# A two-layer block on one core: the triangular inverse in 32x32 blocks, and 64-column products in two halves

## The chip, the cores and the metric

One core of a Trainium2 chip runs the whole kernel as one launch. The metric is device time in microseconds (us), the median of several runs. Engines are named as in the profile: PE (TensorE; PEld are its weight loads), DVE (VectorE), ACT (ScalarE), POOL (GpSimd), SP (SyncE, which issues the loads of weights).

## The reference, cut to what matters

256 tokens of width 1024 pass two layers in fp32. The first has an RWKV-7 mixer and a retention mixer side by side, then a convolutional feed-forward part; the second a Mamba-2 mixer, embeddings and windowed attention. Four places matter here.

- **RWKV-7 recurrence** (8 heads, head width 64). The reference steps through the tokens:

```python
sa = jnp.einsum('bhvk,bhk->bhv', S, -kk_t)
S = (S * w_t[:, :, None, :] + sa[..., None] * (kk_t * a_t)[:, :, None, :]
     + v_t[..., None] * k_t[:, :, None, :])
y = jnp.einsum('bhvk,bhk->bhv', S, r_t)
```

  The kernel does it in two chunks of 128 tokens. In a chunk the vectors `sa` solve a system with a unit triangular 128x128 matrix per head, so the inverse of I minus a strictly triangular matrix is needed for each of 8 heads, twice.
- **Retention**: per chunk of 128 tokens and head, scores q k^T with a decay mask, times v.
- **Mamba-2, diagonal part**: per chunk and head, a masked 128x128 matrix times a 128x64 block (32 heads).
- **Attention**: exponentiated scores (128x128 blocks) times values of 64 columns and a column of ones, 65 together.

## The kernel before, in words

Large products are made from a split: a weight unit of 128x2048 is loaded by SP, ACT writes its rounded upper part (`split_to`, L1321), DVE the rest (L1886), and PE adds three fp32r products (`mm3`, L440 to L442). The small products stay in plain fp32: each such call of `mm` is two weight loads and two passes in the trace, so one product counts as x2. Its operands' first partitions and sizes choose a tile of the PE array: 64 rows by 64 columns, or 64 rows by 128 columns, or all of it.

**Order around the change.** Each engine's program is written out by hand. PE works through `for n in range(2)` (the chunks), from L657 on. Between the small groups stand "dense" quarters (`dense(place)`): each is six fp32r products of 512 columns for the retention's input projection, laid there so that PE has work while ACT and DVE empty the banks. `QUARTERS` says how many stand at each place: one after each group of the inverse, five after the matrices, one or two after `rhs`, `sa` and `y`.

Per chunk:

1. Matrices (L661 to L675): for each of 8 heads two products of 64 rows and 256 columns into a bank (four banks in turn); DVE masks and writes them out (L2172). Two groups `L` (L674) make diagonal 64x64 blocks.
2. Start of the inverse: DVE masks the `L` banks (L2180), masks `invT` (L2183, two instructions of 64 partitions), and adds the unit matrix to both (L2187, 128x1024), which releases `inv_start`. POOL masks the pieces for each level into `lk`, two buffers in turn (L1230, two instructions of 64x512 a level).
3. Levels 1 to 5, on two 64x64 blocks per head held in `inv` and `invT`: `t1` (16 products, helper `blocks`, L654), a dense quarter while ACT copies `t1` to SBUF (L1517), then `x` and `xt` (32 products), a dense quarter while DVE adds them to `inv` and `invT` (L2194, L2197; at level 5 into `invTw`, L2200, L2201). Level 6 joins the two halves (L694, L700).
4. `rhs`, `sa`, `y` (L719, L728, L740, L741, and in the second chunk L716 and L736 of 128 columns): products of 64 columns on the whole array; the first chunk then makes the state (L748, L749).

In the second chunk DVE also does the rotary embedding of the retention's q and k between the levels (`rope_piece`: L2127 to L2131, L2145). Later come the retention scores (`scores_of`, L758), the Mamba diagonal (`diagonal`, L907, 8 groups of 8 products) and the attention's values (`values`, L1094, 12 groups of 4 products).

Of the kernel before, what the change touches and what calls it, by code (L numbers as in the profile page):

```python
# [27 lines left out]
P = 128  # L28
# [8 lines left out]
def constants():  # L37
# [10 lines left out]
    row6, col6 = row % 64, col[:, :64]  # L48
    for k in range(LEVELS - 1):
        same = (row6 >> (k + 1)) == (col6 >> (k + 1))  # L50
        parts[f"off{k}"] = same & (((col6 >> k) & 1) == 1) & (((row6 >> k) & 1) == 0)
    parts["off0L"] = (row6 >> 1 == col6 >> 1) & (col6 & 1 == 0) & (row6 & 1 == 1)
    parts["ident6"] = (row6 == col6)
# [104 lines left out]
def build(nc, io, out, where, ncols):  # L158
    ctx = ExitStack()
    with ctx:  # L160
# [77 lines left out]
        inv, invT, invTw, t1 = ar(23056, 8, 64), ar(23568, 8, 64), ar(24080, 8, P), ar(25104, 8, 64)  # L238
        both_inv, lk = ar(23056, 16, 64), ar(11280, 2, 8, 64)
# [181 lines left out]
        def _(pe):  # L421
# [226 lines left out]

            def blocks(key, bank, a, b):

                ps = take(pe, key, bank)
                for hd in range(8):
                    for r in (slice(0, 64), slice(64, P)):
                        last = mm(ps[r, 64 * hd:64 * hd + 64], a[r, hd, :], b[r, hd, :], start=True, stop=True)  # L654
                fill(last, key)

            for n in range(2):  # L657
# [3 lines left out]
                for hd in range(8):  # L661
                    p, o = hd // 2, hd % 2
                    r = slice(64 * o, 64 * o + 64)
                    ps = take(pe, ("m", n, hd), hd % 4)
                    mm(ps[:, 0:256], bt[r, p, n, :], zr[r, p, n, :], start=True, stop=True)
                    fill(mm(ps[:, 256:512], kt[r, p, n, :], zr[r, p, n, :], start=True, stop=True), ("m", n, hd))
                    if hd in (3, 5):
                        o = hd // 5
                        r = slice(64 * o, 64 * o + 64)
                        ps = take(pe, ("L", n, o), 4 + o)  # L670
                        for p in range(4):
                            for b in range(2):
                                c = slice(64 * b, 64 * b + 64)
                                last = mm(ps[c, 64 * p:64 * p + 64], zr[r, p, n, c], bt[r, p, n, c], start=True, stop=True)  # L674
                        fill(last, ("L", n, o))  # L675
# [3 lines left out]
                for k in range(1, LEVELS - 1):  # L679
                    pe.wait_ge(sem("lk_ready"), 10 * n + 2 * k)  # L680
# [7 lines left out]
                    blocks(("x", n, k), 0, invT, t1)  # L688
                    blocks(("xt", n, k), 1, t1, invT)
                    dense(("x", n, k))  # L690
                emptied(pe, ("x", n, 5))
                ps = take(pe, ("t1", n, 6), 4)
                for hd in range(8):
                    last = mm(ps[64:P, 64 * hd:64 * hd + 64], mats[0:64, hd, 0, 64:P], inv[0:64, hd, :], start=True, stop=True)  # L694
# [19 lines left out]
                for p in range(4):  # L714
                    if n:
                        mm(ps[:, P * p:P * p + P], zr[:, p, n, 0:P], s0[:, p, :], start=True, stop=False)  # L716
                    for o in range(2):
                        hd = 2 * p + o
                        last = mm(ps[:, 64 * hd:64 * hd + 64], mats[:, hd, 2, :], vrow[:, n, 64 * hd:64 * hd + 64],  # L719
                                  start=(n == 0), stop=(n == 0 or o == 1))  # L720
# [3 lines left out]
                if n == 0:  # L724
                    pe.wait_ge(sem("corner_clear"), 1)
# [8 lines left out]
                for p in range(4):  # L734
                    if n:
                        mm(ps[:, P * p:P * p + P], zr[:, p, n, P:2 * P], s0[:, p, :], start=True, stop=False)  # L736
                    for o in range(2):
                        hd = 2 * p + o
                        c = slice(64 * hd, 64 * hd + 64)
                        mm(ps[:, c], mats[:, hd, 3, :], vrow[:, n, c], start=(n == 0), stop=False)  # L740
                        last = mm(ps[:, c], mats[:, hd, 1, :], sa[:, c], start=False, stop=(n == 0 or o == 1))  # L741
# [11 lines left out]
            def scores_of(n):  # L753
                for o in range(2):
                    r = slice(64 * o, 64 * o + 64)
                    ps = take(pe, ("s", n, o), 2 + o)
                    for p in range(4):
                        last = mm(ps[:, P * p:P * p + P], kTr[r, p, P * n:P * n + P], qT[r, p, P * n:P * n + P],  # L758
                                  start=True, stop=True)
                    fill(last, ("s", n, o))  # L760
# [141 lines left out]
            def diagonal(g, n):  # L902
                pe.wait_ge(sem("wT_ready"), 4 * g + 2 * n + 2)
                ps = take(pe, ("yd", g, n), 6 + n)
                for e in range(8):
                    hd = 8 * g + e
                    last = mm(ps[:, 64 * e:64 * e + 64], wT[:, n, e, :], xd[:, n, 64 * hd:64 * hd + 64],  # L907
                              start=True, stop=True)
# [177 lines left out]
            def values(z):  # L1086
# [5 lines left out]
                for e in range(nh):  # L1092
                    for s in range(kt_):
                        last = mm(ps[:, 65 * e:65 * e + 65], aeT[:, z % 2, P * (kt_ * e + s):P * (kt_ * e + s) + P],  # L1094
                                  vv[:, s, 2 * u + o, :], start=(s == 0), stop=(s == kt_ - 1))
# [104 lines left out]
        def _(pool):  # L1200
# [25 lines left out]
            pool.memset(invTw[64:P, :, 0:64], 0.0).then_inc(sem("corner_clear"), 1)  # L1226

            def level_masked(n, k, r):

                pool.tensor_tensor(lk[r, k % 2, :, :], mats[r, :, 0, r], const(f"off{k}")[r].unsqueeze(1).broadcast_to([64, 8, 64]),  # L1230
                                   ALU.mult).then_inc(sem("lk_ready"), 1)

            for n in range(2):
                for k in range(1, LEVELS - 1):
                    if k == 1:
                        pool.wait_ge(sem("mats_ready"), 8 * (n + 1))
                        if n:
                            full(pool, ("t1", 0, 4))
                            full(pool, ("t1", 0, 5))
                    if k > 2:  # L1240
                        full(pool, ("t1", n, k - 2))
                    level_masked(n, k, slice(0, 64))
                    level_masked(n, k, slice(64, P))
# [50 lines left out]
        def _(act):  # L1294
# [217 lines left out]
            for n in range(2):  # L1512
                dense(("L", n), outs_behind=0)
                for k in range(1, LEVELS):
                    ps = full(act, ("t1", n, k))
                    r = slice(0 if k < 6 else 64, P)
                    empty(A(t1[r, :, :], ps[r, :].rearrange("p (a b) -> p a b", a=8), ACT.Copy), ("t1", n, k))  # L1517
# [338 lines left out]
        def _(ve):  # L1856
# [310 lines left out]
            for n in range(2):  # L2167
# [10 lines left out]
                for o in range(2):  # L2178
                    ps = full(ve, ("L", n, o))
                    empty(TT(iv[:, :, o, :], ps[:, 0:256].rearrange("p (a b) -> p a b", a=4),  # L2180
                             bc(const("off0L").unsqueeze(1), P, 4, 64), mul), ("L", n, o))
                for r in (slice(0, 64), slice(64, P)):
                    TT(invT[r, :, :], mats[r, :, 0, r], bc(const("off0")[r].unsqueeze(1), 64, 8, 64), mul) \  # L2183
# [612 lines left out]
```

## Time and profile before

| | us |
|---|---|
| three runs | 923.46, 923.89, 926.66 (median 923.89) |
| the profiled execution, its own time | 921.99 |
| its span | 920.1 |
| PE busy | 887.1 (96% of the span) |
| DVE busy | 671.3 (73%) |
| ACT busy | 505.7 (55%) |
| POOL busy | 88.2 (10%) |

Busy time is the time in which at least one instruction of the engine runs. Passes on different tiles of the array overlap, so the length of a group says more than the mean of one pass. In the timeline a row is a run of like instructions: start, length from the first start to the last end, engine, line, number of records.

### The profile page before, as it was taken

What the parts mean: (1) busy time and instruction counts of PE and PEld (TensorE: products, weight loads), DVE (VectorE), ACT (ScalarE), POOL (GpSimd) and SP (SyncE); (2) the same over time, 40 slices, a digit from 0 to 9 for tenths busy, and PEclk for the clock granted to TensorE, in tenths of its full rate; (3) what the DMA queues carried; (4) which work ended last, traced back from release to release, by engine and by line L of the source; (5) the groups of instructions that cost most, each with busy time, mean ns of one, the idle gap of its engine ahead of it and who ended that gap; (6) DMA issues with size and microseconds to landing.
All of it is one profiled execution on the core that took longest, in us unless ns stands there. A gap on an engine that the chain in (4) does not pass through costs nothing.

```text
span 920.1 us, 15340 instructions
## 1 busy us (share of the span) xinstructions
PE 887.1 (96%) x6217; PEld 768.1 (83%) x6217; DVE 671.3 (73%) x950; ACT 505.7 (55%) x722; POOL 88.2 (10%) x88
## 2 busy tenths in 40 slices
PE   6999999999999989999999899999999998999998
PEld 6997787798878779999988699988888886878777
DVE  6689729947777688888844777887686777776665
ACT  6863332334553567566634566764656566576553
POOL 6004405200000000000000000008220000000000
PEclk9999999999999989999999999999999999999999
DMA  9543322222644456655555365543323544522231
GB/s 306 171 137 98 116 93 93 93 92 92 226 167 147 170 191 205 201 183 188 196 194 193 101 189 184 184 137 122 108 93 108 179 149 176 190 92 92 92 116 68
DMA packets 80984, 136.43 MB, mean 148 GB/s; under 512 B 3958, under 2 KB 46546, under 8 KB 80913
## 3 DMA queue, kind: packets, MB, share of 16 engines
q1 hardware_dynamic: 78800, 130.91, 43.1%
q0 software_dynamic: 2112, 4.53, 1.5%
q8 instruction: 50, 0.82, 0.4%
q14 instruction: 22, 0.17, 0.1%
HBM read 134.38 MB, written 1.05 MB: 147 GB/s over the span
## 4 chain that ended last, share of the span: by engine, by line
PE 79%; DVE 9%; ACT 6%; issue 4%; DMA 2%; SPq 0%; DVEq 0%; ACTq 0%
PE bank L440 21%; PE bank L441 20%; PE bank L442 20%; PE bank L654 3%; PE bank L429 3%; DVE lower L1886 2%; ACT upper L1321 2%; PE bank L1094 1%; PE bank L899 1%; PE bank L907 1%; PE bank L1078 1%; DVE arena L2429 1%; DMA loaded<-in_w_in 1%; ACT arena L1420 1%; DVE arena L2183 1%
## 5 line engine op out<-in xcount | busy, mean ns | idle before, releaser
L1886 DVE TENSOR_TENSOR lower<-loaded,upper 128x2048 fp32r<-128x2048 f32 x122 | 280.8, 2305 | 122.8 <-ACT upper L1321 121.2
L1321 ACT ACTIVATE upper<-loaded 128x2048 fp32r<-128x2048 f32 x122 | 231.9, 1904 | 113.9 <-PE bank L442 93.2
L440 PE MATMUL bank<-xT_upper,upper 128*128 128x256 f32 (+1 forms) x664 | 187.0, 282 | 1.3 <-DVE xT_lower L1951 1.3
L441 PE MATMUL bank<-xT_lower,upper 128*128 128x256 f32 (+1 forms) x664 | 185.5, 279 | 0.0
L442 PE MATMUL bank<-xT_upper,lower 128*128 128x256 f32 (+1 forms) x664 | 185.4, 279 | 0.0
L440 PE MATMUL bank<-upper,xT_upper 128*128 128x512 f32 (+1 forms) x360 | 146.7, 408 | 4.7 <-DVE lower L1886 3.5
L442 PE MATMUL bank<-upper,xT_lower 128*128 128x512 f32 (+1 forms) x360 | 139.9, 389 | 0.0
L441 PE MATMUL bank<-lower,xT_upper 128*128 128x512 f32 (+1 forms) x360 | 139.3, 387 | 0.0
L440 PEld LDWEIGHTS bank<-xT_upper,upper 128*128 128x128 f32 (+1 forms) x664 | 125.8, 190 | 2.4 <-issue 2.2
L441 PEld LDWEIGHTS bank<-xT_lower,upper 128*128 128x128 f32 (+1 forms) x664 | 126.1, 190 | 0.2
L442 PEld LDWEIGHTS bank<-xT_upper,lower 128*128 128x128 f32 (+1 forms) x664 | 125.9, 190 | 0.1
L440 PE MATMUL bank<-upper,split_arena 128*128 128x512 f32 x296 | 121.0, 409 | 2.9 <-DVE split_arena L1951 2.1
L441 PE MATMUL bank<-lower,split_arena 128*128 128x512 f32 x296 | 117.5, 397 | 0.0
L442 PE MATMUL bank<-upper,split_arena 128*128 128x512 f32 x296 | 117.3, 396 | 0.0
L440 PEld LDWEIGHTS bank<-upper,xT_upper 128*128 128x128 f32 x360 | 67.8, 188 | 20.8 <-DVE lower L1886 4.6
L442 PEld LDWEIGHTS bank<-upper,xT_lower 128*128 128x128 f32 x360 | 67.8, 188 | 14.6
L441 PEld LDWEIGHTS bank<-lower,xT_upper 128*128 128x128 f32 x360 | 68.0, 189 | 12.3 <-issue 0.5
L1420 ACT ACTIVATE arena<-bank 128x512 f32<-128x512 f32 (+1 forms) x67 | 37.2, 584 | 62.0 <-PE bank L442 18.1
L440 PEld LDWEIGHTS bank<-upper,split_arena 128*128 128x128 f32 x296 | 55.9, 189 | 17.6 <-DVE lower L1886 2.1
L442 PEld LDWEIGHTS bank<-upper,split_arena 128*128 128x128 f32 x296 | 55.9, 189 | 13.6
L441 PEld LDWEIGHTS bank<-lower,split_arena 128*128 128x128 f32 x296 | 56.0, 189 | 12.5 <-issue 0.5
L429 PE MATMUL bank<-consts,arena 128*128 128x128 f32 (+2 forms) x333 | 49.6, 288 | 15.8 <-DMA arena<-in_norm_mix_pre 5.1
(347 smaller groups left out, 1128.3 us busy)
## 6 DMA issues: line engine op xcount, KB each, us to landing
loaded<-in_w_in SPq DMA_DIRECT2D x26, 1024.0 KB, 5.1
loaded<-in_ffn_w_up SPq DMA_DIRECT2D x22, 1024.0 KB, 5.1
loaded<-in_ssm_in_w SPq DMA_DIRECT2D x20, 1024.0 KB, 5.2
loaded<-in_ffn_w_down SPq DMA_DIRECT2D x11, 1024.0 KB, 4.9
loaded<-in_ssm_out_w SPq DMA_DIRECT2D x8, 1024.0 KB, 5.0
loaded<-in_ple_gate_w SPq DMA_DIRECT2D x8, 1024.0 KB, 5.1
loaded<-in_attn_in_w SPq DMA_DIRECT2D x8, 1024.0 KB, 5.2
loaded<-in_w_branch_ret SPq DMA_DIRECT2D x4, 1024.0 KB, 5.1
```

The source lines that it names most:

```text
L429: last = pe.transpose(ps[0:n, j * P:j * P + m], a, ident[0:m, 0:m])
L440: mm(out, a[0], b[0], start=start, stop=False)
L441: mm(out, a[0], b[1], start=False, stop=False)
L442: return mm(out, a[1], b[0], start=False, stop=stop)
L654: last = mm(ps[r, 64 * hd:64 * hd + 64], a[r, hd, :], b[r, hd, :], start=True, stop=True)
L899: last = mm(ps[:, P * e:P * e + P], later[:, z % 2, e, :], const("incl"), start=True, stop=True)
L907: last = mm(ps[:, 64 * e:64 * e + 64], wT[:, n, e, :], xd[:, n, 64 * hd:64 * hd + 64], start=True, stop=True)
L1078: last = mm(ps[:, w * e:w * e + w], aqT[r, u, nh * gh * n + e, P * n:P * n + P], akT[r, u, 0:w], start=False, stop=(e == nh - 1))
L1094: last = mm(ps[:, 65 * e:65 * e + 65], aeT[:, z % 2, P * (kt_ * e + s):P * (kt_ * e + s) + P], vv[:, s, 2 * u + o, :], start=(s == 0), sto ...
L1321: A(part(upper, PARTS, n), part(loaded, LOADS, n), ACT.Copy).then_inc(uppers, 1)
L1420: empty(A(dst, ps[0:part_, 0:w], func), key)
L1886: TT(part(lower, LOADS, n), part(loaded, LOADS, n), part(upper, PARTS, n).bitcast(F32), sub) \
```

## The change

- Levels 1 to 4 work on four 32x32 blocks per head (32 products where there were 16, each with 32 rows, 32 stationary and 32 moving columns), on the four diagonal tiles of the array; `lk`, `inv`, `invT` and the masks have 32 columns per head. POOL first copies the four diagonal 32x32 blocks to `diag`, and DVE waits for that. POOL's masks are one instruction of 128x256 a level.
- Level 5 joins pairs of 32-blocks: 16 products of 32x32 in each of `t1`, `x`, `xt`, from `mats`, `inv` and `invT`.
- POOL copies the blocks after level 4 into `inv6` (2 copies) and `invTw` (4 copies); DVE copies what level 5 made. PE waits for POOL's six copies (`inv_placed`) ahead of level 6.
- Products of 64 or 65 columns on the whole array (`rhs`, `sa`, `y`, `diagonal`, `values`; with them those of 128 columns in the second chunk's `rhs` and `y`) become two, each with half of the stationary columns (`halves`).
- The matrices and the retention scores are issued for two heads in turn, on the upper and the lower 64 rows; the two `L` groups become one of 32 products, 64 rows by 32 columns.
- The table of constants is 288 columns narrower (664 KB before).

```diff
+            def halves(ps, c, a, b, start, stop):
+                mm(ps[0:64, c], a[:, 0:64], b, start=start, stop=stop)
+                return mm(ps[64:P, c], a[:, 64:P], b, start=start, stop=stop)
...
             def blocks(key, bank, a, b):
                 ps = take(pe, key, bank)
                 for hd in range(8):
-                    for r in (slice(0, 64), slice(64, P)):
-                        last = mm(ps[r, 64 * hd:64 * hd + 64], a[r, hd, :], b[r, hd, :], start=True, stop=True)
+                    for r in fourths:
+                        last = mm(ps[r, 32 * hd:32 * hd + 32], a[r, hd, :], b[r, hd, :], start=True, stop=True)
                 fill(last, key)
...
+                for p in range(4):
+                    mps = [take(pe, ("m", n, 2 * p + o), (2 * p + o) % 4) for o in range(2)]
+                    for o in range(2):
+                        mm(mps[o][:, 0:256], bt[rows_[o], p, n, :], zr[rows_[o], p, n, :], start=True, stop=True)
+                    for o in range(2):
+                        fill(mm(mps[o][:, 256:512], kt[rows_[o], p, n, :], zr[rows_[o], p, n, :], start=True, stop=True),
+                             ("m", n, 2 * p + o))
+                    if p == 1:
+                        lps = [take(pe, ("L", n, o), 4 + o) for o in range(2)]
+                        for p4 in range(4):
+                            for b in range(4):
+                                c = slice(32 * b, 32 * b + 32)
+                                for o in range(2):
+                                    last = mm(lps[o][c, 32 * p4:32 * p4 + 32], zr[rows_[o], p4, n, c], bt[rows_[o], p4, n, c],
+                                              start=True, stop=True)
...
-                for k in range(1, LEVELS - 1):
-                    pe.wait_ge(sem("lk_ready"), 10 * n + 2 * k)
+                for k in range(1, 5):
+                    pe.wait_ge(sem("lk_ready"), 4 * n + k)
...
+                pairs = ((fourths[0], fourths[1]), (fourths[2], fourths[3]))
+                for hd in range(8):
+                    for a, b in pairs:
+                        last = mm(ps[b, 32 * hd:32 * hd + 32], mats[a, hd, 0, b], inv[a, hd, :], start=True, stop=True)
...
+                dense(("x", n, 5))
+                pe.wait_ge(sem("inv_placed"), 6 * n + 6)
...
-                    last = mm(ps[:, 64 * hd:64 * hd + 64], invTw[:, hd, :], rhs[:, 64 * hd:64 * hd + 64],
-                              start=True, stop=True)
+                    c = slice(64 * hd, 64 * hd + 64)
+                    last = halves(ps, c, invTw[:, hd, :], rhs[:, c], True, True)
...
+                for r in fourths:
+                    pool.tensor_copy(diag[r, :, :], mats[r, :, 0, r]).then_inc(sem("diag_ready"), 1)
+                pool.wait_ge(sem("diag_ready"), 4 * n + 4)
+                for k in range(1, 5):
                     if k > 2:
                         full(pool, ("t1", n, k - 2))
+                    pool.tensor_tensor(lk[:, k % 2, :, :], diag[:, :, :], const(f"off{k}").unsqueeze(1).broadcast_to([P, 8, 32]),
+                                       ALU.mult).then_inc(sem("lk_ready"), 1)
...
+                for r in fourths[0:2]:
+                    pool.tensor_copy(inv6[r, :, r], inv[r, :, :]).then_inc(sem("inv_placed"), 1)
+                emptied(pool, ("xt", n, 4))
+                if n:
+                    full(pool, ("sa", 0))
+                for r in fourths:
+                    pool.tensor_copy(invTw[r, :, r], invT[r, :, :]).then_inc(sem("inv_placed"), 1)
...
+                ve.wait_ge(sem("diag_ready"), 4 * n + 4)
+                TT(invT[:, :, :], diag[:, :, :], bc(const("off0").unsqueeze(1), P, 8, 32), mul).then_inc(sem("inv_masked"), 1)
...
-                TT(both_inv, both_inv, bc(const("ident6").unsqueeze(1), P, 16, 64), add).then_inc(sem("inv_start"), 1)
+                TT(both_inv, both_inv, bc(const("ident5").unsqueeze(1), P, 16, 32), add).then_inc(sem("inv_start"), 1)
```

## Rows read from the trace of the kernel before

**Rows 1.** The page: span, busy time by engine, chain that ended last.

```profile
span 920.1 us, 15340 instructions
...
PE 887.1 (96%) x6217; PEld 768.1 (83%) x6217; DVE 671.3 (73%) x950; ACT 505.7 (55%) x722; POOL 88.2 (10%) x88
...
PE 79%; DVE 9%; ACT 6%; issue 4%; DMA 2%; SPq 0%; DVEq 0%; ACTq 0%
```

**Rows 2.** Busy time by stretch: second chunk's levels, Mamba's diagonal, attention.

```profile
core 0: us, PE busy (x) PEld busy (x) DVE busy (x) ACT busy (x) POOL busy (x), PEclk, DMA share, GB/s
...
153.00:185.00 32.00, 32.00 (x551) 25.85 (x545) 29.06 (x34) 10.77 (x11) 11.15 (x7) 1.00 0.31 100
...
634.00:712.00 78.00, 76.11 (x455) 64.94 (x454) 57.74 (x86) 45.74 (x77) 18.63 (x16) 1.00 0.32 108
...
812.00:880.00 68.00, 66.28 (x366) 52.93 (x365) 42.42 (x101) 43.50 (x76) 0.00 (x0) 1.00 0.24 78
```

**Rows 3.** Timeline of PE, second level of the first chunk.

```profile
93.46 1.15 PE L654 MATMUL bank<-arena 64*64 64x64 f32 x32
94.54 0.50 PE L440 MATMUL bank<-upper,xT_upper 128*128 128x512 f32 x1
94.88 0.39 PE L441 MATMUL bank<-lower,xT_upper 128*128 128x512 f32 x1
...
95.80 0.40 PE L442 MATMUL bank<-upper,xT_lower 128*128 128x512 f32 x1
96.13 2.08 PE L654 MATMUL bank<-arena 64*64 64x64 f32 x64
98.14 0.50 PE L440 MATMUL bank<-upper,xT_upper 128*128 128x512 f32 x1
98.48 0.39 PE L441 MATMUL bank<-lower,xT_upper 128*128 128x512 f32 x1
```

**Rows 4.** Timeline of PE: a group on one 64x64 tile; two column tiles, same rows.

```profile
118.53 1.14 PE L694 MATMUL bank<-arena 64*64 64x64 f32 x16
...
75.28 0.68 PE L674 MATMUL bank<-arena 64*64 64x64 f32 x16
```

**Rows 5.** Timeline of PE's weight loads, the 10 ns from 87.18.

```profile
87.18 0.14 PEld L654 LDWEIGHTS bank<-arena 64*64 64x64 f32 x2 [0.78 <-DVE arena L2187]
```

**Rows 6.** Timeline of PE around `sa` of the first chunk, whole array.

```profile
126.69 0.39 PE L442 MATMUL bank<-upper,xT_lower 128*128 128x512 f32 x1
126.92 1.89 PE L728 MATMUL bank<-arena 128*128 128x64 f32 x16
128.62 0.48 PE L440 MATMUL bank<-upper,xT_upper 128*128 128x512 f32 x1
128.94 0.40 PE L441 MATMUL bank<-lower,xT_upper 128*128 128x512 f32 x1
```

**Rows 7.** Mamba's diagonal (all), one group of attention's values, one of the scores.

```profile
L907 PE MATMUL bank<-arena 128*128 128x64 f32 x128 | 15.2, 272 | 0.0
...
820.37 1.11 PE L1094 MATMUL bank<-arena 128*128 128x65 f32 x8
...
221.82 1.71 PE L758 MATMUL bank<-arena 64*128 64x128 f32 x16
```

**Rows 8.** DVE: ahead of the inverse (timeline), second chunk's levels (groups: busy, mean ns).

```profile
79.78 1.29 DVE L2172 TENSOR_TENSOR arena<-bank,consts 128x512 f32<-128x512 f32 x2 [0.50 <-PE bank L666]
...
85.02 2.10 DVE L2187 TENSOR_TENSOR arena<-arena,consts 128x1024 f32<-128x1024 f32 x1
...
L2194 DVE TENSOR_TENSOR arena<-arena,bank 128x512 f32<-128x512 f32 x5 | 3.4, 681 | 1.9 <-PE bank L654 1.9
...
L2128 DVE TENSOR_TENSOR lora<-arena,small 128x256 f32<-128x256 f32 x4 | 3.8, 952 | 0.0
...
L2129 DVE TENSOR_TENSOR lora<-arena,small 128x256 f32<-128x256 f32 x4 | 1.7, 416 | 0.0
```

**Rows 9.** Timeline of POOL: masks for levels 1 and 2, and for level 5.

```profile
81.34 6.92 POOL L1230 TENSOR_TENSOR arena<-arena,consts 64x512 f32<-64x512 f32 x4 [65.42 <-DVEq L2176]
...
100.97 2.63 POOL L1230 TENSOR_TENSOR arena<-arena,consts 64x512 f32<-64x512 f32 x2 [3.27 <-PE bank L654]
```

More of the change, by code:

```diff
@@ L47, in constants @@
     parts["blkret"] = np.repeat(parts["blk"][:, ::64], P, axis=1)
[L48 to L53, printed above, removed]
+    row5, col5 = row % 32, col[:, :32]
+    for k in range(LEVELS - 2):
+        same = (row5 >> (k + 1)) == (col5 >> (k + 1))
+        parts[f"off{k}"] = same & (((col5 >> k) & 1) == 1) & (((row5 >> k) & 1) == 0)
+    parts["off0L"] = (row5 >> 1 == col5 >> 1) & (col5 & 1 == 0) & (row5 & 1 == 1)
+    parts["ident5"] = (row5 == col5)
     lg = np.log1p(-np.exp2(-5.0 - np.arange(8)))
@@ L647, in _ @@
             pe.wait_ge(sem("decayed"), 1)
+            fourths = [slice(32 * g, 32 * g + 32) for g in range(4)]
             def blocks(key, bank, a, b):
@@ L660, in _ @@
                     turns(("kbT", 1), 3, [bt[:, p, 0, :] for p in range(4)])
[L661 to L675, printed above, removed]
+                rows_ = (slice(0, 64), slice(64, P))
@@ new lines, in _ @@
+                for p in range(4):
[13 more added lines that the diff above has]
+                                              start=True, stop=True)
+                                    if p4 == 3 and b == 3:
+                                        fill(last, ("L", n, o))
@@ L693, in _ @@
                 for hd in range(8):
[L694 removed]
+                    last = mm(ps[64:P, 64 * hd:64 * hd + 64], mats[0:64, hd, 0, 64:P], inv6[0:64, hd, :], start=True, stop=True)
                 fill(last, ("t1", n, 6))
@@ L735, in _ @@
                     if n:
-                        mm(ps[:, P * p:P * p + P], zr[:, p, n, P:2 * P], s0[:, p, :], start=True, stop=False)
+                        halves(ps, slice(P * p, P * p + P), zr[:, p, n, P:2 * P], s0[:, p, :], True, False)
                     for o in range(2):
@@ L739, in _ @@
                         c = slice(64 * hd, 64 * hd + 64)
-                        mm(ps[:, c], mats[:, hd, 3, :], vrow[:, n, c], start=(n == 0), stop=False)
-                        last = mm(ps[:, c], mats[:, hd, 1, :], sa[:, c], start=False, stop=(n == 0 or o == 1))
+                        halves(ps, c, mats[:, hd, 3, :], vrow[:, n, c], n == 0, False)
+                        last = halves(ps, c, mats[:, hd, 1, :], sa[:, c], False, n == 0 or o == 1)
                 fill(last, ("y", n))
@@ L753, in scores_of @@
             def scores_of(n):
[L754 to L758, printed above, removed]
+                ps = [take(pe, ("s", n, o), 2 + o) for o in range(2)]
+                for p in range(4):
+                    for o in range(2):
+                        r = slice(64 * o, 64 * o + 64)
+                        last = mm(ps[o][:, P * p:P * p + P], kTr[r, p, P * n:P * n + P], qT[r, p, P * n:P * n + P],
                                   start=True, stop=True)
-                    fill(last, ("s", n, o))
+                        if p == 3:
+                            fill(last, ("s", n, o))
             def outputs_of(n):
@@ L906, in diagonal @@
                     hd = 8 * g + e
-                    last = mm(ps[:, 64 * e:64 * e + 64], wT[:, n, e, :], xd[:, n, 64 * hd:64 * hd + 64],
-                              start=True, stop=True)
+                    last = halves(ps, slice(64 * e, 64 * e + 64), wT[:, n, e, :], xd[:, n, 64 * hd:64 * hd + 64], True, True)
                 fill(last, ("yd", g, n))
```

88 lines of the change are left out of this document (50 added, 38 removed).

## The prediction

> **What bounds the kernel now.** I read the page first: PE is busy for 887.1 of 920.1 us and holds 79% of the chain that ended last [rows 1]. Then the stretches: in the second chunk's levels PE is busy for all of 32 us, in Mamba's diagonal for 76 of 78, in attention for 66 of 68, at a granted clock of 1.00 (2.4 GHz) [rows 2]. So time taken off PE's small groups comes off the end, as long as ACT, DVE and POOL keep up. Of these DVE is near its limit in one place: 29.06 of 32 us in the second chunk's levels [rows 2].
>
> Then the timeline, for the length of the groups. In a level `t1` (x32) stands at 93.46 and the next dense product at 94.54; `x` and `xt` (x64) run from 96.13 to 98.14 [rows 3]. Less the last pass's 0.22 us, 64 passes take 2.08 - 0.22 = 1.86 us, 29 ns each. A group on one tile, x16 in 1.14 us, gives (1.14 - 0.22) / 15 = 61 ns a pass, the first gap being longer; so one 64x64 tile takes a pass about every 58 ns and two tiles share that time fully. The same holds for two column tiles on the same rows: x16 in 0.68 us is 31 ns a pass [rows 4]. Loads of two tiles start almost together: two of them, each 0.13 us, cover 0.14 us in the first 10 ns of a group [rows 5]. Changing the form of tile costs something: from the start of the last dense product (95.80) to that of the second one after (98.48) are 2.68 us; two ordinary steps are 0.46, the 64 passes 64 x 29.2 = 1.87 us, which leaves 0.35 us for going in and out.
>
> Whole-array products of 64 columns: from 126.69 to 128.94 are 2.25 us, less 0.46 is 1.79 us for 16 passes, 112 ns a pass with no visible switch [rows 6]. That is four times the pace of two 64-tiles, for twice the array.
>
> **The change, part by part.** The sum is made against the profiled execution (921.99 us, 1.9 below the median of 923.89); the savings are then taken off the median.
>
> (1) *Levels 1 to 4.* Twice as many passes, half as wide, on four tiles instead of two. No row has a 32-column pass. Bounds: if a tile's pass shrinks with its columns, it takes 32 ns (128 stationary columns take 112 ns [rows 6], 64 take 58.4, so 64 columns are 53.6 and some 5 ns are fixed; 32 columns are 27 and 5), four tiles give 8 ns a pass, and `t1` takes 0.51 us instead of 0.93, `x`+`xt` 1.02 instead of 1.87: 1.27 us off a level. If each pass keeps the 29.2 ns that it has on average now [rows 3], `t1` takes 1.87 and `x`+`xt` 3.74: 2.80 us more a level. I take the first, because the pace of rows 3 and rows 4 is exactly a tile's own time divided by the tiles, and the loads of rows 5 start a few ns apart; nothing there looks like a limit per instruction. For 8 levels: -10.2 us (bound +22.4).
>
> (2) *Level 5.* As many passes as before, 32 wide on two tiles: 16 ns each, again -1.27 us a chunk, -2.5 in all; 0 if the pass does not shrink. Level 6 stays.
>
> (3) *Halves.* 8 products become 32 passes at 29.2 ns, 0.93 + 0.35 for the switch = 1.28 against 1.79: -0.5 us. Nearest row is x16 of two column tiles on 64 rows [rows 4]; on 128 rows it is not shown. `rhs` and `sa` of both chunks: 4 x 0.5. The two `y` have 16 products: 3.57 becomes 1.87 + 0.35, -1.35 each. The 128-column products of the second chunk stay at two loads' worth of time (112 ns a pass, two at a time). Together -4.7. Mamba's diagonal, x128 in 15.2 us [rows 7], is 8 such groups: -4.1. Attention: a group of x8 takes 1.11 us [rows 7], 8 x 112 = 0.90 without the tail; as halves 0.48 + 0.35, some 0.1 less, and part of it is taken up by the wait for ACT's exponentials: -1.2 for 12 groups. Sum -10.0. The bound on the other side, if halves do not share: 32 x 58.4 + 0.35 = 2.22 instead of 1.79 for 8 products, 12 us more over all sites.
>
> (4) *Scores by two heads in turn.* x16 in 1.71 us [rows 7] is one group after the other at 107 ns; with upper and lower rows in turn about 0.95: -0.75 a chunk, -1.5 (bounds 0 and -1.6).
>
> (5) *Matrices and `L`.* PE waits for DVE's masking there (the last two, to 81.07, after a wait of 0.50 [rows 8]). What shrinks is `L`, twice 0.68 us [rows 4] to one group of about 0.5, and part of the interleaving: -0.75 a chunk, -1.5 (bounds 0 and -2.6).
>
> (6) *Start of the inverse.* Now DVE ends the 128x1024 add at 87.12 [rows 8], and PE's loads had been idle for 0.78 us by 87.18 [rows 5]. In the new kernel POOL's four copies come first. No copy of POOL is in the trace; its masks of 64x512 take 1.3 us each when alone (2.63 for two) and 1.7 beside DVE (6.92 for four) [rows 9], 2.6 to 3.4 ns a column, so a copy of 256 columns costs 0.3 to 0.9 us. I take 0.5: from 81.1 the copies end at 83.2, `invT` (0.42) and the add of 512 columns (0.69) at 84.5 (84.5 to 86.1 with 0.9). PE comes there at 87.18 less (5), about 86.2: hidden by the five dense quarters (5 x 6 x 0.23 = 6.9 us), without them it would be 3 us a chunk. Counted 0.
>
> (7) *POOL's six copies ahead of level 6.* They start when DVE has added level 4 and take 6 x 0.5 = 3 us, at most 5.4; PE has three dense quarters (4.1 us), `t1`, `x` and `xt` of level 5 (1.5 + 0.7) ahead of the wait: 6.3 us. Counted 0. Queued behind PE's wait are level 6 and all of `rhs`, so each us over would be lost.
>
> (8) *DVE in the second chunk.* PE's stretch of 32 us shrinks by 5 x 1.27 to 25.7. DVE's 29.06 loses 0.27 for each of nine adds (681 against 416 ns for half the columns [rows 8]), 2.4 us, and part of what POOL's port use costs it: the same instruction takes 952 ns on average at L2128 beside POOL and 416 at L2129 mostly after it [rows 8], and POOL was busy for 11.15 us [rows 2] where about half is left. That makes 23.5 to 24.5 us of 25.7, 93% full. What is late next is DVE's add of `x` ahead of `t1`: I give back 1.5 us there (0 to 4), and 1.5 more for waits of ACT and DVE in all the other shortened groups (0 to 3).
>
> (9) The narrower table: 0.
>
> Sum: -10.2 - 2.5 - 10.0 - 1.5 - 1.5 + 3.0 = -22.7, so 923.9 - 22.7 = **901 us**.
>
> **Rivals.**
>
> *A pass of 32 columns takes as long as one of 64.* Then four tiles give 58.4 / 4 = 14.6 ns a pass; twice the passes at half the time each cancels: (1) and (2) are 0, and less is given back: 923.9 - 13.0 + 1 = 912. For it: the 5 fixed ns are worked out from two sizes, and neither is 32. Against it: nothing in the rows. The Trainium skill ("TensorEngine Tiling (Array Packing)", Instruction Overhead) speaks for it: a matmul has some 60 cycles of overhead, and one should not take the tiling factor from a dimension that is already small. No row here tests that rule.
>
> *PE cannot be fed fast enough (the slower side).* Now at most one load and one pass are asked for in 29.2 ns; (1) asks for four times that, in groups of 64 and 128 passes. With p ns for a pass, 24 products of 64 passes change by 24 x (64p - 934) ns: nothing at 14.6, +16 us at 25, +22.4 at 29.2. With the other parts (-13) the whole breaks even at p = 23 and is over 0.5% slower from p = 26; at 29.2 it is 923.9 - 13.0 + 22.4 = 933. Against it: rows 5, two loads within a few ns, but two are not a stream. The Trainium skill ("TensorE: Matmul & The Clock Gate", "Wait - 56ns, not 53.3ns?") says that start-to-start never drops below about 25 ns; its p would give an estimate of about 927, and rows 5 differ from it for two different tiles.
> Between 10 and 23 ns the same mechanism gives 904 to 924.
>
> *Halves over all 128 rows do not share their time.* Then (3) is +12 instead of -10: 901 + 22 = 923, no change. Against it: two column tiles at 31 ns a pass [rows 4].
>
> **How the numbers follow.** 0.5% (4.6 us) is about what a measurement of this kernel can tell from no change. Forecast (897 to 907): 0.45. Pass that does not shrink: 0.15. Feeding between: 0.15, half of it faster by over 0.5%. Feeding at 26 ns or over: 0.12. Halves not shared: 0.06. Others, of both signs (a granted clock that drops once more or less, a stall behind POOL): 0.07. Faster 0.71, same 0.15, slower 0.14. The range goes from 895, with nothing given back, to 928, which leaves out the slow end alone.
>
> **What would show it.** In the timeline `x`+`xt` should be x128 in about 1.2 us (2.1 for the first rival, over 3.5 for the second), `t1` x64 in 0.7; a diagonal group x32 in about 1.15 instead of x16 in 1.9; the scores' x16 in 1.1. The second chunk's levels should be 6 us shorter with DVE over 90% busy, and PE should show no wait for POOL. Wrong would be a group of 128 passes above 1.9 us, or an idle PE of over 1 us a level behind DVE or POOL.

## The result and the profile after

The new kernel takes 912.97 us (median of 4 runs, 911.06 to 913.91) against 923.67 for the one before (4 runs): 10.7 us less, ratio 0.989, 95% interval 0.987 to 0.991. The prediction was 901, with a range of 895 to 928: the direction and the range held, but less than half of the 22.7 us came. The profiled run took 913.91 us, its span is 912.1. Single executions differ before the change even begins: the transposes ahead of the matrices start at 72.22 us in the profile before and at 74.42 in this one, so a difference of 1 to 2 us between two profiles says nothing by itself.

The page, as [rows 1], with the queue that fetches instructions (before: 50 packets, 0.82 MB):

```profile
span 912.1 us, 17764 instructions
...
PE 865.1 (95%) x7417; PEld 740.6 (81%) x7417; DVE 650.8 (71%) x948; ACT 503.2 (55%) x722; POOL 73.4 (8%) x96
...
q8 instruction: 59, 0.97, 0.4%
...
PE 79%; DVE 7%; ACT 6%; issue 5%; DMA 2%; SPq 0%; DVEq 0%; ACTq 0%
```

PE is busy for 22 us less, but its share falls. The same two stretches as in [rows 2] (columns as there):

```profile
153.00:185.00 32.00, 27.96 (x896) 21.24 (x894) 23.25 (x34) 9.30 (x11) 4.31 (x7) 1.00 0.29 99
634.00:712.00 78.00, 73.03 (x551) 59.80 (x551) 58.45 (x89) 46.51 (x79) 15.97 (x12) 0.98 0.33 112
```

In the levels PE now idles for 4 us of 32, where it idled for none, and DVE, feared at 93%, is busy for 23.25. The timeline of PE, levels 1 and 2 of the first chunk, answers to [rows 3]:

```profile
88.57 0.75 PE L661 MATMUL bank<-arena 32*32 32x32 f32 x64
89.25 0.50 PE L445 MATMUL bank<-upper,xT_upper 128*128 128x512 f32 x1
...
90.83 1.36 PE L661 MATMUL bank<-arena 32*32 32x32 f32 x128
92.12 0.50 PE L445 MATMUL bank<-upper,xT_upper 128*128 128x512 f32 x1
...
93.71 0.59 PE L661 MATMUL bank<-arena 32*32 32x32 f32 x45
97.23 0.53 PE L661 MATMUL bank<-arena 32*32 32x32 f32 x19 [2.94 <-issue]
97.69 0.80 PE L445 MATMUL bank<-upper,xT_upper 128*128 128x512 f32 x1
```

Level 1 is what was forecast: `t1` is 0.68 us long (1.08 before), `x` and `xt` 1.29 (2.01). In level 2 PE stops after 45 of 64 passes for 2.94 us and waits for nothing that the profile shows ("issue"). The second chunk, same view, L661 alone:

```profile
153.46 1.31 PE L661 MATMUL bank<-arena 32*32 32x32 f32 x128
156.29 0.62 PE L661 MATMUL bank<-arena 32*32 32x32 f32 x49
157.84 0.32 PE L661 MATMUL bank<-arena 32*32 32x32 f32 x15 [0.93 <-issue]
159.70 1.13 PE L661 MATMUL bank<-arena 32*32 32x32 f32 x106
161.76 0.38 PE L661 MATMUL bank<-arena 32*32 32x32 f32 x22 [0.94 <-issue]
163.66 0.75 PE L661 MATMUL bank<-arena 32*32 32x32 f32 x64
165.94 1.31 PE L661 MATMUL bank<-arena 32*32 32x32 f32 x128
168.77 0.38 PE L661 MATMUL bank<-arena 32*32 32x32 f32 x23
170.47 0.56 PE L661 MATMUL bank<-arena 32*32 32x32 f32 x41 [1.32 <-issue]
172.56 0.89 PE L661 MATMUL bank<-arena 32*32 32x32 f32 x80
174.30 0.61 PE L661 MATMUL bank<-arena 32*32 32x32 f32 x48 [0.86 <-issue]
```

The waits of PE over the whole run sum these up:

```profile
PE bank L661 <- issue: 7.6, 6, 2.9
```

Six stops: two of the first chunk's eight groups are broken in two (the other stop, of 0.61 us, is in `x` and `xt` of level 4), and four of the second chunk's. Taken from start to next product, the 16 groups of levels 1 to 4 last 25.2 us; unbroken they would last 8 x (0.68 + 1.24) = 15.4, before they lasted 8 x (1.08 + 2.01) = 24.7. Of the 9.8 us between 25.2 and 15.4 the stops are 7.6; the rest is mostly the restart behind each and one group at the lower clock (`x` and `xt` of level 2, 1.86 us instead of 1.24). So all that the narrow tiles save in levels 1 to 4 is lost again. Before the long stop the DMA engines are busy for 80% of the time, and behind it the clock is at its lower level (1.2 GHz) for 5.7 us (windows, columns as [rows 2]):

```profile
91.31:94.86 3.55, 2.98 (x146) 2.29 (x133) 2.66 (x3) 1.60 (x1) 0.00 (x0) 1.00 0.80 259
...
97.20:102.90 5.70, 5.67 (x154) 4.50 (x155) 0.77 (x2) 0.98 (x2) 0.73 (x1) 0.50 0.02 6
```

**Where the stops stand.** Count PE's own instructions in the program's order: an fp32 product is four (two loads, two passes), a split product or a transpose two, a wait one. (A half pass below is a load whose pass comes after the stop.) A level has 410 (218 before). The second level's `t1` begins at instruction 1637; 45 passes further is 1727. The others come out in the same way: 2599 + 2 x 76 = 2751; 4188 + 2 x 49.5 = 4287; 4330 + 2 x 106.5 = 4543; 5009 + 2 x 23 = 5055; 5150 + 2 x 80.5 = 5311. All six leave the remainder 191 when divided by 256. The number of packets fits blocks of that size as well: PE's loads, passes and waits in the trace are 15,174, or 59.3 times 256, and q8 has 59 packets of 16,384 bytes; before they were 12,761, or 49.8 times 256, and 50 packets. Each stop ends 1.2 to 1.5 us after such a packet has ended. Where two stops follow each other on neighbouring blocks, 256 instructions last 161.76 - 157.84 = 3.92 us and 174.30 - 170.47 = 3.83 us. At 3.85 us for 256, a level of 410 takes 6.2 us at the least; the level of before took 6.27, and the four of the second chunk now take 25.2 us, 6.3 each. That is the theory the runs had to test: **PE's instructions come in blocks of 256, asked for one block ahead, one in about 3.85 us at most.** (Pairs of stops in the later profiles lie 3.28 to 4.20 us apart, so the last number is a middle and not a limit.)

### The profile page after: what moved, and what is told of

The parts are those of the page before. It is cut to its first block, busy times and chain, and to the rows that moved or that the text cites. A ratio compares the mean times of both kernels' runs of the same rounds, so it can differ in the third digit from the quotient of the medians.

```text
span 912.1 us, 17764 instructions
## 1 busy us (share of the span) xinstructions
PE 865.1 (95%) x7417; PEld 740.6 (81%) x7417; DVE 650.8 (71%) x948; ACT 503.2 (55%) x722; POOL 73.4 (8%) x96
## 4 chain that ended last, share of the span: by engine, by line
PE 79%; DVE 7%; ACT 6%; issue 5%; DMA 2%; SPq 0%; DVEq 0%; ACTq 0%
PE bank L445 22%; PE bank L447 21%; PE bank L446 21%; PE bank L429 3%; ACT upper L1358 3%; DVE lower L1925 2%; PE bank L440 2%; PE bank L661 2%; PE bank L928 1%; PE bank L1106 1%; DVE arena L2469 1%; DMA h<-in_x 1%; ACT arena L1457 1%; DMA loaded<-in_kv_w 1%; ACT arena L1841 1%
## 5 line engine op out<-in xcount | busy, mean ns | idle before, releaser
L447 PEld LDWEIGHTS bank<-upper,xT_lower 128*128 128x128 f32 x360 | 68.0, 189 | 14.7
```

The source lines that it names most:

```text
L447: return mm(out, a[1], b[0], start=False, stop=stop)
```

## The experiments

Times are medians; ratios are against the kernel before in the same session (922.7 to 923.6 us).

**One part undone at a time.** In levels_64 `blocks` goes over two slices of 64 again and level 5 is in its loop, with all that POOL and DVE did for the levels before; the halves and the new order of scores and matrices stay:

> All parts of the change but the levels: halves, the scores' and the matrices' new order stand, levels 1 to 5 are the two 64x64 blocks per head of before. Theory (PE's instructions come in blocks of 256, and levels 1 to 4 of the new kernel use them faster than they come, so the stalls eat what the narrow passes save): the levels' saving of about 11 us and the stalls of about 11 us go together, so 910 to 915, no gap over 0.5 us in the middle of any level, and the half-clock stretch at 96 us is gone. Rival 1 (DVE and POOL hold the new levels back): the same time, but PE's waits for them go away. Rival 2 (the levels do save their 11 us and the loss of 12 us against the forecast lies elsewhere): 922 to 925.

914.26 us (ratio 0.991, 0.988 to 0.993), and no stop inside a level. In the stretch in which the new kernel works through levels 1 to 4 of the second chunk, PE never idles:

```profile
151.20:176.40 25.20, 25.20 (x444) 20.35 (x442) 23.85 (x25) 7.88 (x8) 11.21 (x7) 1.00 0.27 86
```

The new kernel has 21.16 us of PE in those 25.20. So the narrow levels are worth 1 to 2 us, not 12.7, and the rest of the change is worth about 9.4.

In halves_whole `halves` is one product: `return mm(ps[:, c], a, b, start=start, stop=stop)`.

> The new kernel with each product of 64 (or 128) columns over the whole array again one product; levels, scores and matrices stay new. From the two traces: 0.6 us in each of four groups of 8 products, 1.4 in each of the two y groups, 0.5 in each of 8 diagonals, 0.29 in each of 11 attention groups, 12.5 us in all; so 924 to 926, about what the kernel before takes. If the halves are worth what step 3 of the prediction said (10.0), 923. If part of their gain is taken back by waits of ACT and DVE behind them, under 919.

927.69 us (1.004, 1.001 to 1.006): 14.7 more than the new kernel. That is more than the groups give. The blocks now end elsewhere, and its profile has three stops of 3.2 to 3.6 us instead of one of 2.9, and 11.5 us of "issue" instead of 7.6; that this makes up the difference is likely and not shown by itself.

**Count or tile form?** In levels_64_nops and levels_64_more each head of `blocks` is followed by `pe.nop()` (8), or by `pe.nop().then_inc(sem("more"), 1)` (16):

> The kernel levels_64 with 64 empty instructions of PE spread over each group of 16 products of levels 1 to 5, so a level has as many instructions as in the new kernel (432 instead of 240) but no tile of 32 and no pass more. Theory (supply): gaps of 1 to 3 us appear in the middle of groups, each ending 1 to 1.5 us after an instruction packet, and it takes 8 to 20 us more than levels_64 beside what the empty instructions take one by one. Rival (32-wide tiles are what stalls): groups are evenly longer or as before, no such gaps, 910 to 918.

914.08 us with the same 16088 instructions as levels_64: the empty instructions never reached the chip. It only repeats levels_64.

> The kernel levels_64 with 16 empty instructions of PE that count up a semaphore (those without one are dropped from the program when it is built, which is why levels_64_nops had the 16088 instructions and the time of levels_64) behind each head of the groups of levels 1 to 5: 624 instructions a level instead of 240, no 32-wide tile. Theory (supply): a block lasts 2.6 us where 3.7 are needed, so gaps in the middle of the 64x64 groups, at positions of PE's stream that are equal modulo 256, 20 to 30 us in sum: 934 to 945, beside what the empty instructions take by themselves. Rival (32-wide tiles are what stalls): no gaps, groups evenly longer at most.

1457.89 us: 16 of them take 2.25 us between two heads, 140 ns each. That hides any supply; nothing follows for the theory. Then real products of one column behind each of seven heads of a group, `mm(PS[5][r, 0:1], a[r, hd, :], b[r, hd, 0:1], ...)`, six a head:

> The kernel levels_64 with extra real products of PE in levels 1 to 5: behind each of the first seven heads of a group six more products of the same 64x64 blocks, of one column each, whose results nobody reads: 744 instructions a level instead of 240, and still no tile of 32. Theory (supply by count of instructions): a block of 256 lasts about 2.4 us in x and xt, so gaps of 0.5 us and more stand in the middle of the 64x64 groups, all at positions with the remainder 191 modulo 256. Rival (tiles of 32 are what stalls): groups are evenly longer, no gap inside one. The time itself says little, since the extra products take 30 to 50 us.

1079.76 us, no stops, but the kernel never asked fast enough: 12 passes of one column take 0.32 us, and the 64-column ones 0.14 for four:

```profile
93.77 0.46 PE L662 MATMUL bank<-arena 64*64 64x1 f32 x12
94.09 0.31 PE L659 MATMUL bank<-arena 64*64 64x64 f32 x4
```

16 passes with their loads in 0.47 us are 14.6 ns an instruction, 3.7 us for 256: about what can be supplied. From 97.5 us on, for 34.1 us, the granted clock was 0.50, and the kernel asked more slowly still. A stop without a tile of 32 was therefore not seen. What speaks against the tiles is the place of the stops. In shift, 128 such empty instructions stand ahead of the inverse:

> The new kernel with 128 empty instructions that count up a semaphore in front of the inverse, where they are hidden by or add at most 1 to 3 us to the wait that stands there. Theory (supply): the gaps move to other places of the program, half a block earlier than now (positions 1727, 2239, 2495, 4287, 4799, 5055 in the new stream, all with the remainder 191), of about the same sum: 911 to 916. Rival (a gap belongs to a group, as a conflict over a buffer or a bank would): they stay in t1 of level 2 and x of level 4 of the first chunk, and in t1 and x of levels 2 and 4 of the second.

931.98 us, where 911 to 916 had been expected: those 128 took 16.3 us by themselves. The stops moved as the count demands. All six positions named beforehand have one (that at 4799 of 0.17 us only), and 2751 and 3007 have one besides. In the first chunk four stand in groups that had none, and the one in `x` and `xt` of level 4 comes after 12 passes instead of 76 (timeline of PE; 13 of 128 passes left is 1496 + 2 x 115.5 = 1727):

```profile
108.70 0.32 PE L663 MATMUL bank<-arena 32*32 32x32 f32 x13 [0.68 <-issue]
...
117.39 0.45 PE L663 MATMUL bank<-arena 32*32 32x32 f32 x32 [0.99 <-issue]
...
121.06 0.54 PE L663 MATMUL bank<-arena 32*32 32x32 f32 x39 [0.75 <-issue]
...
126.30 1.21 PE L663 MATMUL bank<-arena 32*32 32x32 f32 x116 [0.59 <-issue]
```

All again have the remainder 191. A conflict over a buffer, or a tile that stops by itself, would have stayed at its place in its group.

**Work between the groups.** (The expectations count a quarter as 24 instructions; it has 12, so a level is 410, not 432, before 218, and 422 with one more quarter.) In moved, `QUARTERS[("x", n, k)] = 2` for k of 1 to 4, `("L", 1)` 4 and `"end"` 1:

> The new kernel with the same instructions, but eight of the 80 dense quarters stand elsewhere: a second one behind x and xt of levels 1 to 4 of each chunk; they come from the end (8 becomes 1) and from in front of the second chunk's inverse (5 becomes 4). Theory (instruction supply): a level asks for 456 instructions in 6.4 us instead of 432 in 5.0, so most of the 11.3 us of stalls is filled by products that have to be done anyway: 903 to 907, mid-group gaps under 4 us in sum. Rival (tiles of 32 themselves stop now and then, whatever stands between): the stalls stay, 911 to 914. Rival (the place at the end was needed, or DVE becomes the bound in the second chunk with the quarters' splits): 914 to 920, with waits of PE for DVE or ACT.

911.72 us (0.988, 0.986 to 0.990), not to be told from the new kernel, though 903 to 907 had been expected; "issue" fell to 4.8 us. `x` and `xt` are 256 instructions in a row, more than a quarter behind them can make good. In spread that quarter stands between the two (`dense(("xm", n, k))`):

> As the run moved, but the second quarter of each of the levels 1 to 4 stands between x and xt instead of behind xt: level = t1 (128 instructions), quarter (24), x (128), quarter, xt (128), quarter. Theory (supply, now with its rule: PE's instructions arrive in blocks of 256, a block is asked for when PE enters the one before it and is there 3.7 us later): every 256 instructions in a row now last about 3.6 us or more, so no gap over 0.3 us inside a group of the levels, no clock drop behind one, and it beats the kernel after by 6 to 9 us, less 8 more switches of tile form at 0.3: 903 to 908. Rival (32-wide tiles stop by themselves): the gaps stay, 910 to 914. Rival (the moved quarters cost at the end what they save): no gaps, yet 910 to 915.

910.4 us (0.984, 0.981 to 0.987). Its profile has no stop in a level, and PE idles nowhere in the stretch of before:

```profile
151.20:176.40 25.20, 25.20 (x757) 18.87 (x744) 16.27 (x26) 9.52 (x11) 4.93 (x6) 1.00 0.39 129
```

In between the quarter that is there anyway is moved:

> The new kernel with the quarter that stood behind xt in levels 1 to 4 set between x and xt; no quarter comes from elsewhere, so a level has its 432 instructions in 5.0 us as before. Theory (supply): what counts is the mean rate and not the order, the gaps stay, 5 to 8 us in sum but in other groups (xt and t1 now follow each other), plus up to 2 us for switches: 911 to 916. Rival (PE waited for ACT's copy or DVE's add after all, which now have a quarter more of time): 903 to 908.

919.2 us (0.995, 0.992 to 0.998), slower than expected, with 9.1 us of "issue" in seven stops. So the order alone does not help. Nor does the lower rate alone do it: moved and spread have the same instructions in a level, and only spread puts a quarter between any two groups. Both kernels again, side by side:

> The new kernel once more, to stand beside the three that follow on one chip: 911 to 914. In its profile again the six gaps inside groups of levels 1 to 4 at positions of the same remainder modulo 256, 5 to 12 us in sum (theory: supply of instructions); if they are at other remainders or missing, the theory falls.

> The kernel spread once more. Theory (supply): no gap inside the levels, 4 to 8 us below after_again, 905 to 909. Rival (its gain over the new kernel was chance): within 2 us of after_again.

912.11 (0.987, 0.984 to 0.990) and 910.44 (0.984, 0.981 to 0.988). The stops of after_again are at the same positions, 8.9 us in seven; spread_again has two at remainder 191 (1.7 and 1.1 us) and a trace of a third where spread had none. The gain of spreading is 1.7 us, below the forecast of 4 to 8 and less than the two intervals can tell apart (single runs of spread_again go from 905.67 to 913.54): fewer stops are shown, a shorter time hardly. One kernel's stops differ from run to run.

**What makes a stop long.** In the profiles there are eight stops of 3 us and over. Each belongs to a packet that starts 3.7 to 4.3 us after the block before was entered, and in that time the DMA engines are 75 to 85% busy; with quiet engines a packet in the levels starts after about 1 us (0.7 to 1.4). So two weight loads were held (SyncE waits for the fill of `t1`, level 2, ahead of them):

> The new kernel with SyncE holding back two weight loads (the 1 MB that starts at 90.9 us, and the one at 151.3) until t1 of the second level is done; nothing else moves. In all profiles so far an instruction packet that started within 1.3 us of its block's turn had quiet DMA engines ahead of it or in part, and of those that came over 2.4 us late 15 of 16 in the levels had the engines 83 to 100% busy. Theory (contention: packets of instructions queue behind the weights on the same DMA engines): the gap at position 1727 falls from 3.1 to 3.9 us to under 1.3, the one at 4287 from 1.1 to 1.7 to under 0.9, the half-clock stretch at 96 us goes, the other gaps stay; 2 to 6 us below after_again, 906 to 910, unless the held loads meet the next packets. Rival (the delay is the sequencer's own): the gap at 1727 stays over 3 us, same time within 1 us.

911.19 us (0.986, 0.983 to 0.989). The stop at 1727 is 0.67 us where it was 2.94 and 3.75, with quiet engines ahead of it. The clock stays up in this chunk (in the second it is at 0.50 for 3.4 us from 168.2, behind a stop of 1.6). The four stops of the chunk are now alike, and the two pairs are 3.82 and 3.56 us apart:

```profile
94.11 0.37 PE L661 MATMUL bank<-arena 32*32 32x32 f32 x19 [0.67 <-issue]
97.93 0.41 PE L661 MATMUL bank<-arena 32*32 32x32 f32 x26 [0.83 <-issue]
...
106.11 0.59 PE L661 MATMUL bank<-arena 32*32 32x32 f32 x46 [0.78 <-issue]
109.67 0.65 PE L661 MATMUL bank<-arena 32*32 32x32 f32 x52 [0.61 <-issue]
...
90.47:91.50 1.03, 1.03 (x99) 0.99 (x88) 0.54 (x2) 1.03 (x1) 0.00 (x0) 1.00 0.00 0
```

So instruction packets do queue behind the weights. The time fell by 0.9 us only, which is within the runs' spread, and stayed above the 906 to 910 expected: "issue" is still 6.0 us in seven stops, since those with quiet engines stay.

**Mamba's diagonal.** PE waits there once for DVE's scaled rows (waits of PE, 640 to 690 us, new kernel; before it was 1.4 us, for the same line, then L2513):

```profile
PE bank L429 <- DVE arena L2553: 3.4, 1, 3.4
```

Whole products there again (the `mm` of before in `diagonal`), on top of spread:

> The kernel spread with Mamba's diagonals as whole products again (8 groups, 0.5 us of PE each). Theory: these 4 us reach the end only in part, because PE then comes earlier to the turns of the third group's rows and waits there for DVE (3.61 us instead of 1.64, in every kernel with halves), and the clock falls for some us behind the longer wait: the whole is 0 to 3 us above spread_again, with the wait back at 1.64. Rival (step 3 of the prediction: all of it is worth its time): 4 to 5 us above.

909.44 us (0.984, 0.982 to 0.987), 1.0 below spread_again, with the wait at 1.4. So the halves there gave nothing that can be measured. Scaling before weighing (`group_scale(g - 1)` ahead of `weigh(z + 1)`) in step 13:

> The kernel spread with one exchange on DVE: in step 13 of the diagonal it scales the rows of the third group before it weighs the next step (two products of 0.7 to 0.8 us), so PE's wait for the scaled rows ends 1.5 us earlier. Theory (that wait takes back part of the halves' gain): the wait falls from 3.61 to about 2.1 us, and 1.5 to 4 us are gained, the latter if the clock no longer falls behind it. Rival (the next wait is for what DVE now weighs later): the same time as spread_again, within 1 us.

910.55 us, wait unchanged: the step was misread, the wait belongs to step 10. Halves only where `g > 1`, behind the wait, and then the exchange in step 9:

> The kernel spread with Mamba's diagonals whole in the first two groups of heads (before the wait for the scaled rows) and in halves in the last two (behind it). Theory (the wait eats what is saved ahead of it, nothing eats what is saved behind it): the wait is 1.6 us and not 3.6, and the time is 1 to 3 us below spread and 1.5 to 2 below spread_diag_whole: 906 to 909. Rival (DVE and ACT hold the last two groups too): the time of spread_diag_whole, 909 to 910.

> As late_halves, with the exchange on DVE at the right step: the run spread_scale_first made it in step 13, but the wait stands in step 10 and its rows are scaled in step 9. Here step 9 scales before it weighs. Theory: ACT's root is ready 1.2 us before DVE scales, so the wait falls from 1.6 us to about 0.4 and 0.5 to 1.2 us are gained on late_halves. Rival (the weighing is late next): within 0.5 us of late_halves.

907.97 us (0.983, 0.980 to 0.986), wait 2.0, and **906.06 us** (0.980, 0.977 to 0.984), wait 1.2. Both waits are longer than expected (1.6 and 0.4, in a count that makes this wait 0.2 us longer than the rows here). The second is 17 us faster than the kernel before, and by the ratios of two sessions about 6 faster than the new one. The single steps from spread to it, 1 to 2 us each, are no larger than the spread of the runs. Holding the two loads in it as well:

> The kernel late_halves_scale with the same two loads held until t1 of the second level is done. Theory (contention): the last two gaps (0.9 us at position 1727, 1.6 at 4287) go, and with them their share, 1 to 2.5 us: 903 to 906, unless a held load delays a later packet by as much. Rival: the same time as late_halves_scale, gaps in place.

906.51 us (0.982, 0.979 to 0.985), no gain. The stops at 1727 and 4287 are gone, but the packet for 2751 now came late: it started 3.95 us after the block before was entered, with the DMA engines 80% busy in between:

```profile
114.89 0.26 PE L664 MATMUL bank<-arena 32*32 32x32 f32 x7 [3.35 <-issue]
```

## Why the prediction was right and where it failed

(1) *Levels 1 to 4, -10.2.* This is the step that failed. The pace of a pass was right (128 in 1.24 us, 9.7 ns; 8 forecast), but the saving of 0.40 and 0.77 us a level, 9.4 in all, came back as 9.8 us: 7.6 of stops, the rest mostly restarts and the lower clock. The sentence that failed is "nothing there looks like a limit per instruction": [rows 3] to [rows 5] show two passes at a time, and nobody had asked how many instructions a level has and how they reach PE. The page had the count (q8, 50 packets in 920 us). The closest pair of packets before, 5.1 us apart (169.24 and 174.30), was never read; it would not have shown the limit, but that one is near, since 410 instructions in the 5.1 us of an unbroken level need a packet in 3.2. The second rival had named the place: put into its formula, the mean pace with stops, 25.2 us / 1536 passes = 16.4 ns, gives 24 x (64 x 0.0164 - 0.934) - 13.0 + 923.9 = 913.7 us. Its middle part, "between 10 and 23 ns", to which 0.15 was given, is what happened, though by a supply of blocks and not by a distance from pass to pass. The first rival's number, 912, is as near, and that is chance: its mechanism, a narrow pass as long as a wide one, is not what the timeline shows.
Of the two rules of the Trainium skill held against the sum, the first ("TensorEngine Tiling (Array Packing)", Instruction Overhead) did not decide: the passes on 32x32 tiles do come faster than by that rule (9.7 against 14.6 ns), though on 64x64 tiles one moving column takes nearly as long as 64 (27 ns in levels_64_tiny, 29 in [rows 3]), much as that section says of 1 and 60. The second ("TensorE: Matmul & The Clock Gate", "Wait — 56ns, not 53.3ns?"), that start-to-start never drops below about 25 ns, does not hold for passes on different tiles, by the same 9.7 ns.

(2) *Level 5, -2.5.* Right: 1.08 and 2.01 us became 0.62 and 1.03, 1.44 a chunk.

(3) *Halves, -10.0.* The groups gave more than forecast (halves_whole puts all of them at 14.7 us, longer stops included): a group of 8 products fell from 1.70 to 1.08 us, the two `y` by 1.5 each, attention by 0.3 a group (0.1 forecast). But Mamba's 4.1 us were lost, mostly around one wait, for ACT's root and DVE's scaling, 35 us into the stage; step (8) had given back 1.5 us for all such waits together. This one alone went from 1.4 to 3.4 us. From the group of 16 passes ahead of the stage (615.87 us before, 609.99 now) to the first product behind the wait (675.86 and 669.70), 59.99 us became 59.71. From there to the last transposes (711.46 and 705.77), 35.60 became 36.07: the clock is now at 0.50 for the 3.4 us behind the wait, and before it was not. spread_diag_whole bears out that what is saved ahead of the wait is lost (without the halves the wait is 1.4 us again and the time no longer); that what is saved behind it stays is what late_halves points to, by 1.5 us, less than the runs' spread.

(4), (5) *Scores and matrices, -3.0.* Scores x16 in 1.16 us instead of 1.71, 0.55 a chunk (0.75 forecast); the matrices 0.4 a chunk, and PE's wait for DVE's add behind them, 0.35 a chunk, is gone. About right.

(6), (7), (9) *Nothing from POOL and the table.* Right: DVE's add ends at 86.47 us (85.45 + 1.02) and PE comes at 88.57, and no wait of PE is for POOL.

(8) *DVE, +3.0.* Wrong in its place: DVE was no limit in the levels (23.25 of 32 us, where 23.5 to 24.5 of 25.7 were forecast, and the levels did not get shorter).

Two slips of the working change no term. A whole-array pass at 112 ns is a quarter of the pace of two 64-tiles, not four times it. And the sum with nothing given back is 923.9 - 25.7 = 898, not 895. The direction and the range held because the rest of the change gave 9.4 us (levels_64), about the 13.0 less 3.0 that the sum had for it; of the 12.7 of (1) and (2) 1 to 2 us arrived.

## What to carry to other kernels

Before a loop is cut into more and shorter instructions, count the engine's instructions over 4 us and compare with the packets of its instruction queue: here every 256 of PE's took 3.3 to 3.9 us to come with quiet DMA engines, so a stretch denser than some 66 to 78 a microsecond pays for what it saves with stops. Long independent products among such groups, one between any two, took most stops away here, though hardly any time; and look at what the DMA engines carry when a block is asked for. A time saved ahead of a wait for another engine, as in Mamba's stage, is worth nothing until that wait's chain is shortened too.

## What the runs showed of the hardware

- Instructions of PE arrive in packets of 256 on the same DMA engines as the weights. In the levels a packet starts about 1 us (0.7 to 1.4) after the block before it is entered when the engines are quiet, takes 0.9 to 1.4 us, and its first instruction runs 1.2 to 1.6 us after that; behind a 1 MB weight load it starts up to 4.3 us after (after_again). That it is asked for at about that time is inferred from these numbers. The Trainium skill ("Runtime: NRT & Kernel Launch", Instruction fetch mechanics) says that the fetch goes in blocks of 256, with which the traces agree, and that "ifetch is hidden by the ~20-cyc/instr NX issue floor", which they contradict: PE runs 256 instructions in 1.24 us (`x` and `xt` of a level) and stands still where the next block has not come.
- The clock can fall with a stop: in the new kernel's first chunk it was at 0.50 for the 5.7 us behind the stop of 2.94 us; in after_again, behind 3.75 us, the mean of the next 6.1 us was 0.72; in after_held, behind 0.67 us, it stayed at 1.00.
- On 64x64 tiles a pass of one column takes 27 ns (two tiles in turn, levels_64_tiny), one of 64 columns 29: the moved columns do not set the time there. That a narrower tile helps by its shorter load follows from it, but no run changed the load alone.
- An empty instruction of PE that counts up a semaphore takes 0.13 to 0.14 us.
- Why some packets come late though nothing else is on the DMA engines (one, of shift, after 3.9 us, where it did no harm) is open; so is a stop without tiles of 32, which no kernel here could ask for.
